# Two mixers of a hybrid decoder: last groups in another order, joined GLA chunks, and one convolution tap on ScalarE

## What is computed

```python
# GLA, per chunk of 64 tokens and head; b = cumsum of log gates within the chunk
scores  = where(causal, (q*exp(b - b_mid)) @ (k*exp(b_mid - b)).T, 0)
o       = scores @ v + (q*exp(b)) @ state
state   = state*exp(b_last) + (k*exp(b_last - b)).T @ v
o = rmsnorm(o, g_norm per head) * silu(r);  out = o @ w_out
# SSD
xbc = silu(conv4(xbc) + conv_b)     # depthwise over time: taps t-3, t-2, t-1 and t
y   = (cb * decay * dt) @ x + c @ state * exp(cs) + d_skip * x
y   = rmsnorm(y * silu(z), per group) ;  out = y @ w_out
```

## Time and profile before

| | us |
|---|---|
| median of 3 runs | 1189.26 (1186.78 to 1190.22) |
| the profiled execution's own time | 1189.44 |
| its span | 1187.7 |
| TensorE busy | 1123.2 (95%) |
| TensorE weight loads busy | 950.9 (80%) |
| VectorE busy | 738.4 (62%) |
| ScalarE busy | 631.4 (53%) |
| GpSimd busy | 52.2 (4%) |
| mean granted TensorE clock | 0.969 of full |

### The profile page before, as it was taken

The page is one execution under the profiler, slowest core; times in us unless marked ns, Lnnn a source line. Parts: engine busy times, 40 slices in busy tenths (PEclk is TensorE's granted clock), DMA queues, the critical chain, the costliest instruction groups (busy, mean ns, idle before and its releaser), DMA issues. The chain is left out here.

```text
span 1187.7 us, 16534 instructions
## 1 busy us (share of the span) xinstructions
PE 1123.2 (95%) x5904; PEld 950.9 (80%) x5904; DVE 738.4 (62%) x1174; ACT 631.4 (53%) x978; POOL 52.2 (4%) x81
## 2 busy tenths in 40 slices
PE   6899999969979999999999997999999969999997
PEld 5688888858848888888888885889999957888886
DVE  4545555756657555557655545698999885655554
ACT  6444445664437444447544445577677746544443
POOL 3000000000000000000000000211211100000000
PEclk9899999989979999999999998899999978999999
DMA  7756554443445655553766534484544504855530
GB/s 244 248 178 211 183 170 133 134 134 115 142 142 175 223 178 176 184 190 118 250 203 198 177 106 137 155 272 144 172 144 143 176 15 147 282 192 177 176 127 35
DMA packets 162877, 199.24 MB, mean 168 GB/s; under 512 B 6372, under 2 KB 145856, under 8 KB 162832
## 3 DMA queue, kind: packets, MB, share of 16 engines
q1 hardware_dynamic: 160144, 190.34, 49.4%
q0 software_dynamic: 2384, 7.72, 1.9%
q10 hardware_dynamic: 304, 0.61, 0.1%
HBM read 197.56 MB, written 1.08 MB: 167 GB/s over the span
## 5 line engine op out<-in xcount | busy, mean ns | idle before, releaser
L1362 PE MATMUL ps<-ws,xT 128*128 128x512 f32 x2160 | 502.3, 391 | 6.2 <-DVE ws L979 6.2
L1362 PEld LDWEIGHTS ps<-ws,xT 128*128 128x128 f32 x2160 | 404.6, 188 | 93.8 <-DVE ws L979 8.0
L1381 PE MATMUL ps<-ws,hT 128*128 128x512 f32 x1344 | 337.8, 402 | 4.0 <-DVE hT L1223 3.9
L1381 PEld LDWEIGHTS ps<-ws,hT 128*128 128x128 f32 x1344 | 253.5, 192 | 59.1 <-issue 6.8
L979 DVE TENSOR_TENSOR ws<-raw,ws 128x1024 fp32r<-128x1024 f32 x180 | 218.3, 1223 | 117.1 <-ACT ws L592 116.9
L897 DVE TENSOR_TENSOR ws<-raw,ws 128x2048 fp32r<-128x2048 f32 x90 | 206.8, 2298 | 99.1 <-ACT ws L532 98.7
L592 ACT ACTIVATE ws<-raw 128x1024 fp32r<-128x1024 f32 x180 | 188.3, 1060 | 145.3 <-PE ps L1362 141.7
L532 ACT ACTIVATE ws<-raw 128x2048 fp32r<-128x2048 f32 x90 | 171.1, 1913 | 58.6 <-PE ps L1381 52.4
L1414 PE MATMUL ps<-xT,ws 128*128 128x256 f32 x960 | 119.3, 284 | 0.3 <-ACT feat L538 0.3
L1414 PEld LDWEIGHTS ps<-xT,ws 128*128 128x128 f32 x960 | 116.4, 192 | 0.9 <-DVE ws L897 0.5
L992 DVE TENSOR_TENSOR hT<-ps,hT 128x256 fp32r<-128x256 f32 x88 | 33.7, 420 | 87.0 <-ACT hT L606 86.9
(11 more groups left out here) (196 smaller groups left out, 632.8 us busy)
## 6 DMA issues: line engine op xcount, KB each, us to landing
raw<-in_ffn_w_down SPq DMA_DIRECT2D x88, 512.0 KB, 4.3
raw<-in_ffn_w_gate SPq DMA_DIRECT2D x86, 512.0 KB, 4.0
raw<-in_ffn_w_up SPq DMA_DIRECT2D x86, 512.0 KB, 5.0
raw<-in_ssd_w_in SPq DMA_DIRECT2D x48, 512.0 KB, 4.7
raw<-in_gla_w_in SPq DMA_DIRECT2D x24, 512.0 KB, 4.7
raw<-in_ssd_w_out SPq DMA_DIRECT2D x16, 512.0 KB, 4.2
raw<-in_gla_w_out SPq DMA_DIRECT2D x8, 512.0 KB, 4.8
exps<-cs_rows POOLq DMA_DIRECT2D x8, 512.0 KB, 8.9
```

Source lines behind the costliest of these rows:

```text
L1362: mm = pe.matmul(ps[:, bank + t, :].rearrange("p (s n) -> p s n", s=2), xT[:, k, a, t * P:(t + 1) * P], ws[:, 0:2, b, k * UW:(k + 1) * UW] ...
L1381: mm = pe.matmul(ps[:, 2 * t + n, :], hT[:, par, j, a, t * P:(t + 1) * P], ws[:, slot, b, off:off + 512], start=(first and j + a + b == 0) ...
```

## The change

Four parts.

1. GLA's chunks are joined in pairs through the first chunk's state: `decayed` rescales one chunk's keys and queries each, so that two pairs of chunks become tiles of 128 with one state between them. The state update is one matmul instead of three, the part within chunks two full ones instead of four, the part from the state one instead of three; the scores get two more 64x64 products, and the mask multiply is two operations.
2. The end of both mixers is reordered. The last group's P3 unit is split into two halves, with the last group's row transposes and scores between them (`ahead`); ScalarE and VectorE no longer split the next FFN's first gate/up pair in body n-1 but later, in body n, n+1 and the boundary; the product of group n-2 with `w_out` stands whole before the last group's; the last group's inverse root uses ScalarE's Sqrt and one Newton step.
3. In SSD, ScalarE writes each projected channel tile twice: to `feat`, and times the current token's tap to `ca` (`features_out`); VectorE's `convolution` adds three taps.
4. In SSD's last projected body VectorE's second convolution stands ahead of the state copy, and in both last scans the split of `hT` (`transposed(C)`) stands before the state copy.

```diff
+            def features_out(slot, count, g, c0, done):
+                for j in range(2):
+                    c = c0 + j
+                    tile = 2 * g + c if c < 2 else g + 8 * c
+                    act.wait_ge(tile_mm[slot], count * 2 + j + 1)
+                    act.activation(feat[:, c, CONV - 1:], ps[:, A + j, 0:T], ACT.Copy)
+                    act.activation(ca[:, c, :], ps[:, A + j, 0:T], ACT.Copy,
+                                   scale=pcol[:, 0, bass.ds(tile + 32 * (CONV - 1), 1)]).then_inc(done, 1)
...
                     if scan and ssd:
                         act.wait_ge(e_mm, g - 1 + G + 1)
-                        act.activation(bcb[:, :], ps[:, C, 0:384], ACT.Copy).then_inc(e_out, 1)
-                    if scan and not proj:
-                        transposed(A)
-                    if isinstance(g, int) and g == n - 1:
-                        for q in range(NQ):
+                        act.activation(bcb[:, :], ps[:, B if tail else C, 0:384], ACT.Copy).then_inc(e_out, 1)
+                    if tail:
+                        for q in range(2):
                             gate_up_hi(gate_units_before(ph + 1), q, ph + 1)
-                    elif proj:
+                        p3_tile(n - 1, 1, A)
+                        if ssd:
+                            gate_silu()
+                        act.activation(DUMMY, EPS_COL[1.0], ACT.Sqrt)
+                        transposed(C)
+                    elif proj and not ahead:
...
                 for o in which:
-                    dve.scalar_tensor_tensor(out=fm[:, o, :], in0=ca[:, o % 2, :], scalar=1.0 if o % 2 else P ** -0.5,
+                    if o < 2:
+                        part(o, 0, 0, T).then_inc(feat_done, 1)
+                        continue
+                    near, far, through = (3, 0, 2) if o == 2 else (0, 3, 1)
+                    step.start(part(o, far * CH, near * CH, CH))
+                    part(o, CH, CH, 2 * CH)
+                    step.wait()
+                    dve.tensor_scalar(fm[:, o, near * CH:(near + 1) * CH], fm[:, o, far * CH:(far + 1) * CH],
+                                      edl[:, 0, bass.ds(4 * g + through, 1)], None, ALU.mult).then_inc(feat_done, 1)
...
-                for k in range(CONV):
+                for k in range(CONV - 1):
...
+                    if tail:
+                        y, mh, a = sm[:, 18:20], sm[:, 22:24], sm[:, 20:22]
...
+                        dve.wait_ge(root_y, 4 if ssd else 2)
+                        step(dve.reciprocal(y, sm[:, 26:28]))
+                        step(dve.tensor_tensor(a, y, y, ALU.mult))
+                        step(dve.tensor_tensor(a, a, mh, ALU.mult))
+                        step(dve.scalar_tensor_tensor(out=y, in0=a, scalar=1.5, in1=y, op0=ALU.add, op1=ALU.mult))
...
-                        for c, (bank, o) in () if ssd else ((0, (E, 0)), (2, (E, 256)), (1, (C, 0))):
-                            r, t = slice((c % 2) * CH, (c % 2 + 1) * CH), c // 2
-                            mm = pe.matmul(ps[:, bank, o:o + 256], xw[r, t, 0:P], vs[r, t, :], start=True, stop=True,
+                        else:
+                            pe.matmul(ps[:, E, 0:256], xw[:, 0, 0:P], vs[:, 0, :], start=True, stop=True,
...
+                            for t in range(NT):
+                                pe.matmul(ps[:, A + t, 0:256], wm[:, t, 0, :], vs[:, t, :], start=True, stop=(t == 0),
...
-                    if scan and not proj:
-                        add_output(n - 2, (0,))
-                    if proj:
+                    if tail:
+                        add_output(n - 2)
+                    if ahead:
+                        split(SLOT_P3, g + n0[SLOT_P3])
+                        pe.wait_ge(state_done, G + g if ssd else g)
+                        token_tiles(SLOT_P3, C, (0,))
+                        pe.wait_ge(feat_done, 4 * (g + G) + 2)
+                        rows(g)
+                        pe.wait_ge(y_out, 2 * (g - 1 + G) + 2)
+                        scores(g, B)
+                        token_tiles(SLOT_P3, A - 1, (1,))
```

More of the change, by code:

```diff
@@ L466, in _ @@
             step(pool.memset(ones[:, :], 1.0))
[L467 to L469 removed]
+            step(pool.memset(wm[CH:P, :, 0, 0:CH], 0.0))
             step(pool.memset(feat[:, :, 0:CONV - 1], 0.0))
@@ L788, in body, with gate_silu @@
                     first = isinstance(g, int) and g == 1
-                    if scan:
+                    ahead = isinstance(g, int) and g == n - 1
+                    tail = scan and not proj
+                    def gate_silu():
                         if not first:
@@ new lines, in body @@
+                            past = tri[:, CH:P].rearrange("p (t i) -> p t i", t=1).broadcast_to([P, NT, CH])
+                            dve.tensor_tensor(wm[:, :, 0, CH:P], scores[:, :, CH:P], past, ALU.mult).then_inc(w_done, 1)
+                            past = tri[0:CH, 0:CH].rearrange("p (t i) -> p t i", t=1).broadcast_to([CH, NT, CH])
+                            dve.tensor_tensor(wm[0:CH, :, 0, 0:CH], scores[0:CH, :, 0:CH], past, ALU.mult).then_inc(w_done, 1)
+                    if tail and not ssd:
+                        transposed(C)
@@ L1273, in body @@
                     if proj:
-                        if ssd:
+                        if ssd and not ahead:
                             dve.wait_ge(p2_out, c0 + 2)
                             convolution(g, 2)
-                        else:
+                        elif not ssd:
                             decayed(g, c0, (1, 3, 0))
+                    if tail and not ssd:
+                        lo(*out_unit(g - 1, n, n0))
                     if scan:
@@ L1679, in body @@
                         add_output(n - 1, (0,), True)
-                        add_output(n - 2, (1,))
                         add_output(n - 1, (1,), True)
-                    if scan and not proj:
-                        transpose_rows(A)
+                    if tail:
+                        pe.wait_ge(p3_out, 2 * (g - 1 + G) + 1)
+                        transpose_rows(C)
                     if scan:
```

238 lines of the change are left out of this document (127 added, 111 removed).

## The result

The changed kernel takes 1170.01 us (median of 4 runs, 1167.69 to 1171.55), the kernel before 1189.74 on the same chip (1186.78 to 1190.90). The profiled execution took 1167.69 us (span 1165.8) at a mean TensorE clock of 0.979.

What follows compares the result with a forecast made beforehand. TensorE, busy 95% of the span, was taken as the bound through its instructions, tail gaps and the half clock after them. 4.1 - 1.7 + 9.5 + 5.1 = 17.0 us off 1189.44 gave 1172.4, range 1169 to 1177 (chance 0.60).

Steps and rivals of the forecast that it cites:

- rival A: Both tails: the clock stays up, 6.7 us more gained than forecast, 1166 us; chance 0.13.
- GLA loop, 4.1 us: GLA groups: joined chunks save 3.2 us in two groups and 1.4 in the first, less 0.5 for `decayed`.
- Second write, 1.7 us lost: SSD loop: TensorE waits 0.26 us per body for ScalarE's second write before P2, six bodies and 0.1 in the first.
- Rival C: SSD bodies: ScalarE's extra writes make TensorE wait for `wm`; slower, 1193.5 us at 3 us per body; chance 0.04.
- SSD tail, 9.5 us: End of the SSD mixer: reordering gains 8.4 us up to the last output products and 1.1 from there to the FFN.
- T0: Time mark in each mixer's tail: start of the last P3 unit, 950.77 us in SSD and 320.63 in GLA before.
- S: Time mark in each mixer's tail: start of the last stretch of output products, 983.07 us in SSD before.
- the 0.7 charged for the extra quarter split in the boundary: Before the FFN: VectorE's 1.22 us quarter split precedes the second half's post norm, of which 0.7 us was charged.
- GLA tail, 5.1 us: End of the GLA mixer: reordering takes last P3 start to FFN from 36.8 to 31.7 us, half clock included.
- The forecast's own sign of being wrong: Both tails: the prediction counted itself wrong if, among other signs, the clock there stayed at 1.00.
- Rival B: Both tails: the gaps only move, eating half of the tails' 14.6 us gain, giving 1180 us; chance 0.19.
- Rival D: Both tails: bound by the post norm chain whatever the order, so no change, 1188 us; chance 0.04.

Runs made afterwards that it cites:

- chunks only: The kernel before with GLA's joined chunks alone, tails, convolution and roots as before: 1183.35 us, ratio 0.9946.
- three other kernels with the same GLA code: Changed kernel with the convolution back on VectorE, 1169.28 us; with the tap read from SBUF, 1169.15; with GpSimd's side products behind the root, 1170.44.
- nine zero products: TensorE multiplies zeros before the products needing `hT`; at half clock in the tail-filled kernel with 12 of group n-2's output products moved back behind the last transposes: 1166.79 us.
- zero products in most gaps: Changed kernel with TensorE multiplying zeros in the tails, before GLA's first P2, at SSD's start, in the first FFN and at the very start: 1157.63 us.

## Why the prediction was right, step by step

The median, 1170.01, lies in the forecast's range (1169 to 1177), and the order of the gains is the one forecast. The profiled execution, 1167.69, lies below that range and nearer to rival A.

**GLA loop, 4.1 us.** Right: 4.49, bodies of 26.05 as forecast (26.1), and the kernel with chunks only shows it alone.

**Second write, 1.7 us lost.** The mechanism is shown (the wait goes, and 0.23 us with it, when the bank is read once, with ScalarE's work unchanged), the size a little high: 1.00 us from P1's end to P2's start, not 1.05, so 6 x 0.23 = 1.4 in the bodies and 1.1 in the stage, since the first scanned group got 0.3 us shorter. That VectorE's time was free holds in the loop and not in this first group, whose `wm` TensorE waits for. Rival C is refuted: the bodies grew by no more.

**SSD tail, 9.5 us.** Right in its steps: the root started at T0 + 4.5 (4.6 forecast), its rows were done at T0 + 9.4 (9.8), the wait was 2.4 us (3.0), the 3.38 us wait went but for 0.20, S came at T0 + 22.7 (23.9). The forecast's 5.2 us beside GpSimd was 4.8. Most of the 1.2 us up to S is a shorter stretch of half clock: the first 16 products took 2.75 us, not 3.65 as before, and the state product was done at T0 + 14.1 (15.8); the 24 products behind it took 5.8 us, not 5.4. The stretch to the FFN was 10.05, not 10.8: the 0.7 charged for the extra quarter split in the boundary cost nothing. VectorE makes it from 972.59 on, when TensorE is already at its last output products, and the FFN starts at 972.92 without a wait:

```profile
972.59 1.22 DVE L1012 TENSOR_TENSOR ws<-raw,ws 128x1024 fp32r<-128x1024 f32 x1
```

**GLA tail, 5.1 us.** The term that was mis-sized: it measured 8.6. The forecast charged 1.6 us of half clock ahead of S and 1.2 behind it, and the 0.7 for the split, and none of the three came. This is rival A, in one mixer. The forecast's own sign of being wrong, the clock at 1.00 in the tails, came true in GLA and not in SSD. Behind S the clock doesn't stay up in each execution: in three other kernels with the same GLA code it fell there, and S to FFN took 9.9 to 10.0. With 10.0 the error of this term would be 2.1 us, not 3.5.

**The clock.** What the earlier trace rows showed, a fall to 0.82 with 2.5 us idle in 14, was read as a rule for gaps of this size; the runs show it as something that may or may not happen: the GLA tail after, with 2.1 us idle between 325 and 333, stayed at 1.00, SSD's fell from 949 on behind 2.44 us of wait in one piece, and GLA's fell in three other traces behind the same 1.93 us of wait behind which it stayed up in this one. The Trainium skill (TensorE: Matmul & The Clock Gate, What's actually happening) ties a fall to a whole idle window. The GLA tail agrees with it; read as strictly as for rival A it would have kept the clock up in the other cases too, and there the traces decide against it.

**The sum.** The span fell by 21.9 us, 4.9 more than the forecast 17.0. The first FFN cost 1.4 us more in this execution, which no edit explains: over the traces its first 48 products take 11.2, 12.8 or 14.0 us, in kernels with the same code there. Without it the difference would be 6.3: 3.5 of the GLA tail, 1.9 of the SSD tail, 0.6 of the second write and 0.4 of the GLA loop, all in the same direction. The median lies only 2.4 below the forecast, 2.3 above the profiled execution; that it comes so close is in part luck. The forecast charged half clock in GLA's tail that the trace doesn't have, and the three other executions are slower at a lower mean clock (0.975 and 0.976 instead of 0.979), in stages that no trace shows. Rival B (the gaps only move, 1180) is refuted as a whole: the waits of 4.65, 2.65 and 3.38 us became 2.44, none and 0.20. Rival D (no change) is refuted by the tails.

## What to carry to other kernels

Where an engine is busy 95% of the time and its clock falls behind gaps, price a gap twice: the wait, and the work behind it at half clock. Keep the engine busy with harmless work in gaps that cannot be closed; here that was worth 12 us, nearly as much as the other parts gave beside the joined chunks (some 13). Count that work to the gap at full clock: nine zero products that ran at half clock held up what stood behind them for 1.6 us. And before shortening the work ahead of a wait, look at what ends the wait: work shortened in front of one that another engine sets only makes the gap longer. Here 0.23 us a body was won by reading the bank once, and no total showed it.

## What the runs showed of the hardware

- Half-clock stretches differ between executions of one kernel, and its scatter goes with them: 1162.92 us at a mean clock of 0.985 and 1170.68 at 0.976, the same kernel on the same chip. With zero products in most gaps five runs lie within 2.8 us, at 0.995 to 0.998.
- VectorE's steps on two columns take 0.16 us alone, 0.58 beside GpSimd's product of 128x256 and 0.97 beside that of 128x512; GpSimd's product of 128x512 takes 1.04 us beside such steps and 1.49 beside VectorE's two multiplies of 128x512, which then take 1.71 instead of 1.29.
- A second write from the same PSUM tile takes ScalarE 0.47 us, starts 0.1 us before the first ends, and delays the next unit's first product by 0.21 us (0.30 in the last body), the body by 0.23.
